# Four loads of GpSimd behind the input's landing, memory attention one step earlier, the closing sum of squares behind the up tile

## What is computed

```python
for i in range(DEPTH):                      # DEPTH = 2
    h = rmsnorm(x, mix_norm[i])
    mem_k, mem_v = split(rmsnorm(mem, mem_norm) @ w_mem_kv[i])
    if i == 0:                              # gated short convolution
        b_gate, c_gate, u, q_mem = split(h @ a_in[0])
        y_main = b_gate * causal_short_conv(c_gate * u, conv_w[0])
    else:                                   # stick-breaking attention over shared k, v
        q_sb, q_mem = split(h @ b_in[0])
        y_main = stick_breaking_attention(q_sb, k_sh, v_sh)
    y_mem = softmax(q_mem @ mem_k.T / 8) @ mem_v          # 4 heads of 64, 256 memory rows
    x = x + concat(y_main, y_mem) @ w_o[i]
    h = rmsnorm(x, ffn_norm[i])
    x = x + (silu(h @ w_gate[i]) * (h @ w_up[i])) @ w_down[i]     # 2816 wide
    if i == 0: k_sh, v_sh = split(rmsnorm(x, kv_norm) @ w_kv_shared)
```

## Time and profile before

| | us |
|---|---|
| median of 3 runs | 1225.7 |
| lowest and highest | 1224.52, 1225.96 |
| the profiled execution | 1227.68 |
| its span | 1226.3 |

### The profile page before, as it was taken

The page is one execution under the profiler, slowest core; times in us unless marked ns, Lnnn a source line. Parts: engine busy times, 40 slices in busy tenths (PEclk is TensorE's granted clock), DMA queues, the critical chain, the costliest instruction groups (busy, mean ns, idle before and its releaser), DMA issues.

```text
span 1226.3 us, 21837 instructions
## 1 busy us (share of the span) xinstructions
PE 1163.0 (95%) x9014; PEld 1114.4 (91%) x9014; DVE 832.8 (68%) x1266; ACT 623.4 (51%) x938; POOL 162.1 (13%) x123
## 2 busy tenths in 40 slices
PE   7999899999898789999999999999999998999996
PEld 6989899999887669999999898989899988999995
DVE  4577677778773656777778657386645767677775
ACT  4645544435563546444445665565436544555553
POOL 1102100000120003000000000000001032433431
PEclk8999999999998979999999999999999997999999
DMA  8545578777643125777887445354325553555540
GB/s 300 166 150 186 182 259 267 241 252 226 244 149 113 61 76 174 256 242 248 275 266 240 169 154 170 121 161 149 121 73 167 183 181 103 172 177 194 180 156 36
DMA packets 60467, 221.90 MB, mean 181 GB/s; under 512 B 6752, under 2 KB 7008, under 8 KB 59984
## 3 DMA queue, kind: packets, MB, share of 16 engines
q1 hardware_dynamic: 59904, 219.06, 54.2%
q10 hardware_dynamic: 288, 1.05, 0.2%
q0 software_dynamic: 176, 0.39, 0.2%
HBM read 219.42 MB, written 1.05 MB: 180 GB/s over the span
## 4 chain that ended last, share of the span: by engine, by line
PE 81%; DVE 10%; ACT 5%; issue 3%; DMA 1%; POOL 0%; SPq 0%; ACTq 0%; DVEq 0%
PE PS L350 23%; PE PS L352 22%; PE PS L351 22%; PE PS L355 13%; DVE w_lo L1310 3%; ACT w_hi L837 2%; DVE PS L1879 1%; DMA ARENA<-memT 1%; ACT ARENA L926 1%; DVE SQ L1577 1%; DVE ARENA L1346 0%; DVE raw L1332 0%; PE PS L453 0%; DVE SQ L1346 0%; DVE ARENA L1493 0%
## 5 line engine op out<-in xcount | busy, mean ns | idle before, releaser
L1310 DVE TENSOR_TENSOR w_lo<-raw,w_hi 128x1024 fp32r<-128x1024 f32 x325 | 398.8, 1227 | 277.1 <-ACT w_hi L837 276.6
L837 ACT ACTIVATE w_hi<-raw 128x1024 fp32r<-128x1024 f32 x356 | 372.8, 1054 | 150.7 <-PE PS L352 122.7
L350 PE MATMUL PS<-Y_hi,w_hi 128*128 128x256 f32 x1240 | 359.4, 290 | 11.8 <-DVE w_lo L1310 4.8
L351 PE MATMUL PS<-Y_lo,w_hi 128*128 128x256 f32 x1240 | 354.8, 286 | 0.0
L352 PE MATMUL PS<-Y_hi,w_lo 128*128 128x256 f32 x1240 | 354.7, 286 | 0.0
L350 PEld LDWEIGHTS PS<-Y_hi,w_hi 128*128 128x128 f32 x1240 | 241.8, 195 | 18.4 <-issue 9.7
L351 PEld LDWEIGHTS PS<-Y_lo,w_hi 128*128 128x128 f32 x1240 | 242.2, 195 | 0.4 <-issue 0.2
L352 PEld LDWEIGHTS PS<-Y_hi,w_lo 128*128 128x128 f32 x1240 | 242.0, 195 | 0.0
L350 PE MATMUL PS<-H_hi,w_hi 128*128 128x256 f32 x808 | 232.2, 287 | 7.2 <-POOL H_lo L1936 2.8
L352 PE MATMUL PS<-H_hi,w_lo 128*128 128x256 f32 x808 | 229.3, 284 | 0.0
L351 PE MATMUL PS<-H_lo,w_hi 128*128 128x256 f32 x808 | 229.3, 284 | 0.0
(11 more groups left out here) (210 smaller groups left out, 1342.7 us busy)
## 6 DMA issues: line engine op xcount, KB each, us to landing
raw<-stream SPq DMA_DIRECT2D x404, 512.0 KB, 4.1
ARENA<-memT SPq DMA_DIRECT2D x2, 512.0 KB, 9.2
X<-xT SPq DMA_DIRECT2D x1, 1024.0 KB, 12.9
ARENA<-c_rows SPq DMA_DIRECT2D x2, 512.0 KB, 7.4
ARENA<-memT SPq DMA_DIRECT2D x1, 1024.0 KB, 9.1
ARENA<-ctxT SPq DMA_DIRECT2D x1, 1024.0 KB, 7.0
outT<-ARENA SPq DMA_DIRECT2D x2, 512.0 KB, 2.6
CROW<-c_rows SPq DMA_DIRECT2D x1, 512.0 KB, 8.3
```

Of the source, the lines that this page charges most:

```text
L350: pe.matmul(o, wh, xh, start=start, stop=False, skip_group_check=True)
L351: pe.matmul(o, wh, xl, start=False, stop=False, skip_group_check=True)
L837: act.activation(w_hi[n % RING][:], raw[at][:], ACT.Copy).then_inc(*mark("hi", n))
L1310: dve.tensor_tensor(w_lo[n % RING][:], raw[raw_of("slot", n)][:], w_hi[n % RING][:], ALU.subtract).then_inc(*mark("lo_dve", n))
```

## The change

The first step of memory attention's wait is taken out on all three engines (TensorE's `nothing(6)` becomes `nothing(5)`, ScalarE and VectorE lose their first empty `yield`); `residual_sum` goes from between the first gate and up tile to behind the up tile, in both layers; GpSimd waits for `x_in` before its four loads. No instruction other than that wait is added, and none is removed.

```diff
@@ memory_attention, TensorE
                 for b in bs:
                     emptied[b] = [("ma_exp", l, 7)]
-                yield from nothing(6)
+                yield from nothing(5)
                 pe.wait_ge(*past("ma_prob", l, 7))
@@ gate_up and ffn, TensorE
-            def gate_up(l, j, ready=None, side=None, between=None):
+            def gate_up(l, j, ready=None, side=None):
                 p = j % 2
                 claim(2 * p, 2 * p + 1)
                 assert n == gate_slot(l, j)
                 tall(PS[:, 2 * p, 0:T], H_of[l], ready)
                 emptied[2 * p] = [("gate", l, j)]
-                if between:
-                    between()
                 if side:
                     side.step()
                 tall(PS[:, 2 * p + 1, 0:T], H_of[l])
@@
             def ffn(l, tail):
-                gate_up(l, 0, [("h_lo", l, k) for k in range(KC)], between=lambda: residual_sum(l))
+                gate_up(l, 0, [("h_lo", l, k) for k in range(KC)])
+                residual_sum(l)
                 gate_up(l, 1)
@@ memory_attention, ScalarE
                 yield
-                yield
                 act.wait_ge(*past("ma_max", l))
@@ pool_program
+            pool.wait_ge(*past("x_in"))
             for i, (dst, src) in enumerate(((mask_sb[:], masks), (scan_m[:], scan_mask), (W2[0:RANK, :], gla_w2[0]),
                                             (W2[32:32 + RANK, :], gla_w2[1]))):
                 pool.dma_start(dst, src).then_inc(*mark("second_in", i, by=16))
```

## The result

| | us |
|---|---|
| before, median of 12 runs | 1225.13 |
| after, median of 12 runs | 1229.67 (1226.52 to 1232.42) |
| after / before | 1.0038, 95% interval 1.0029 to 1.0046 |
| profiled execution of after, its span | 1232.05, 1230.7 |

The change costs 4.5 us by the medians and 4.7 by the ratio (3.6 to 5.6), 4.6 in what follows. Against the profiled execution of before the span of after is 4.4 us longer, at a mean clock of 0.976 against 0.978, so the two profiles can be compared place by place.

What follows compares the result with a forecast made beforehand. TensorE bounds the kernel (81% of the chain that ended last). 5.9 + 5.4 - 1.4 - 0.4 + 0.1 - 1.1 = +8.5 on the median of 1225.7 gives 1234.2 us; range 1228.6 to 1238.4.

Steps and rivals of the forecast that it cites:

- the rival of the kept clock: Feed-forward, both layers: TensorE keeps full clock behind both longer stalls, so 5.4 goes: 1228.8 us; chance 0.13.
- the clock behind the two stalls: Third gate tiles, both layers: matmuls at 1.2 GHz for 5.5 us after each restart, 2.7 each, 5.4 together.
- the gains of the other parts: Start 1.4 off, memory attention layer 0 0.4 off, layer 1 net 0.1 on, stick-breaking groups 1.1 off.
- The stalls of TensorE: Before third gate tiles 2.49 to 5.43 and 1.54 to 4.48; before attention's transposes 1.2 in layer 0, 7.3 in layer 1.
- to read "issue" by the code: Third gate tile, both layers: the wait is for the bank that `G_lo` frees, 0.1 before the tile starts.
- part 1: Closing sum behind the up tile: ScalarE's chain to `G_lo` moves by 2.94 a layer, 5.9 together, plus 5.4 of clock.
- 2.49 kept it and 2.69 did not: TensorE's clock after idle time in before's trace: full speed after 2.49 us, 1.2 GHz after 2.69 (at 1034.21).
- The loads: Start: GpSimd's four loads behind the input's landing let the memory halves and the input land earlier; 1.4 us off.
- Memory attention, layer 1, and the groups: Layer 1: 3.0 lost at the transposes, a 3.0 tile given back, net 0.1 on; groups' tails earlier, 1.1 off.
- The tile came back as said: Stick-breaking groups, layer 1: one tile of 3.0 us fills TensorE's 4.65 us idle gap before the third group's tails.
- the two after them keep their distance: Stick-breaking groups: the tails after the third come at 432.1 instead of 433.25, the next two at unchanged distance; 1.1 off.
- The luck of the clock: Other places, such as 1034.21: the clock may be lost or kept as arrival times shift, up to 2.7 us each way.

Runs made afterwards that it cites:

- the kernel without the sum: Against before: GpSimd's loads wait for the input and memory attention's step is taken out, the closing sum not moved; 0.9964, 4.5 us faster.
- the filled gap: Against before: seven matmuls of constants into a free bank in TensorE's idle time ahead of the third stick-breaking group's tails, nothing moved; 0.9963, 4.5 us faster.
- the filled stall of the feed-forward: Against before: closing sum moved behind the up tile, seven matmuls of constants ahead of the third gate tile, both layers; 1.0045, 5.9 us slower.
- layer 1's filled attention stall: Against before: loads' wait, attention's step out, sum inside first gate tile, fourteen warm-up matmuls, eleven matmuls of constants ahead of layer 1's transposes; 0.9915, 1216.46 us.

## Why the prediction was right, and where its sizes were off

The forecast was +8.5, measured +4.6 (3.6 to 5.6): the sign, the mechanisms and the stalls came as worked out, the time at the lower end of the range. By the time alone the result lies nearest to the rival of the kept clock (1228.8), but the trace refutes it: the windows behind both stalls stand at 0.50, and matmuls there are 0.21 apart. Of the 3.9 us between forecast and result, about 1.4 is the clock behind the two stalls, 5.4 forecast and some 4 measured. About 1.7 are the gains of the other parts, 2.8 forecast and 4.5 measured (loads and attention without the sum). The rest, 0.8, lies within the intervals.

**The stalls of TensorE** were read right to about a tenth where it mattered: 5.43 and 4.48 forecast, 5.37 and 4.42 found; 7.3 against 7.11 in layer 1's attention. In layer 0's attention it was 1.2 against 0.86. The step that carried this was to read "issue" by the code: a claim whose bank comes free 0.1 before the tile starts, twice. After the change the profile itself names `G_lo`.

**The clock behind the two stalls was mis-sized**: 5.4 in the sum of part 1, some 4 measured. The step that failed is the one that took 5.5 us at 1.2 GHz after each restart, from memory attention's stall of 4.24. A stretch at 1.2 GHz costs nothing while TensorE is idle, and here more of it lay in the stall. In layer 0 the clock fell near 136.9 (the mean of 136 to 138 is 0.72, so 0.56 of it, the last 1.1 us, at 0.50) and rose near 143.7 (0.57 in 142 to 144). From the restart at 139.88 that is 3.8 us, which cost 1.67. In layer 1 it rose later, 5.1 us behind the restart, and cost 2.25. The prediction gave a bound of 0 to 5.5 and took a value near the top of it. It also rounded up: at the spacings of the rows, 0.12 and 0.21, its 5.5 us cost 2.4 and not 2.7. One profile is thin ground for such a price: in the kernel with the sum alone, memory attention's stall was 4.13, and the matmuls behind it were slow for 3.0 us instead of 5.5.

**"2.49 kept it and 2.69 did not"** held for the one profile and is no line between the two. The stall of 2.49 at the start of layer 0's feed-forward stands unchanged in eight kernels. Six kept the clock at the restart (one of these lost it 1.5 us later). In the kernel without the sum and in that with the filled gap it lost the clock, in the first of these so:

```profile
136.73 0.55 PE L350 MATMUL PS<-H_hi,w_hi 128*128 128x256 f32 x1 [2.49 <-issue]
```

Two other kernels kept it behind 2.73 and 2.78 us of idle time at the place of 1034.21. So some executions of before may already pay a part of the clock's price.

**The loads**: 1.4 forecast, 1.8 measured, 2.4 in the profile. Between the two profiles the landing moved by 1.3, over all profiles by about 1.0. The further 1.0 of the pair, which came from the clock, is mostly the luck of one execution: the first matmuls are at 2.4 GHz in most kernels that leave the loads alone.

**Memory attention, layer 1, and the groups**: 1.4 forecast for all of the attention, 2.0 (0.9 to 3.8) measured. The tile came back as said, with 1.17 idle before the third tails and these at 1.99. From the first group's tails to the last's it takes 40.3 us in four of five profiles of the old order that have no filler in the gap (38.8 in the fifth). The new order was profiled six times: four times it takes 38.1 to 38.6, so 1.7 to 2.2 less, and in after and in the kernel with the attention alone 36.6 and 35.6. The forecast was 1.1. Its step that "the two after them keep their distance" held in the four (to 0.1 us in three of them) and failed in the two. In the four all three tails behind the third ran slow, in the kernel with layer 1's step alone out so:

```profile
429.34 3.43 PE L355 MATMUL PS<-ARENA,consts 128*128 128x256 f32 x12 [1.38 <-DVE ARENA L1501]
435.56 3.63 PE L355 MATMUL PS<-ARENA,consts 128*128 128x256 f32 x12 [1.94 <-DVE ARENA L1501]
442.00 3.25 PE L355 MATMUL PS<-ARENA,consts 128*128 128x256 f32 x12 [2.80 <-DVE ARENA L1501]
```

In after the second of them was at 2.4 GHz, 1.99 instead of 3.59. So the 3.1 in the bookkeeping holds some luck. TensorE's idle time over attention and groups together is the same in both profiles, 17.97 before and 18.31 after: what was won between them is clock alone, and the matmuls of constants won 4.5 of the same kind without moving anything.

**The luck of the clock** was named with up to 2.7 each way. The profile of after shows one such place, in the second block, which the change doesn't touch. Transposes there, in before, in the kernel with the attention alone, in after, and in the kernel with the sum alone:

```profile
813.30 1.09 PE L594 MATMUL PS<-consts,ARENA 128*128 128x128 f32 x8 [2.55 <-DVE ARENA L1586]
```

```profile
803.10 1.09 PE L594 MATMUL PS<-consts,ARENA 128*128 128x128 f32 x8 [2.57 <-DVE ARENA L1584]
```

```profile
816.27 1.97 PE L593 MATMUL PS<-consts,ARENA 128*128 128x128 f32 x8 [2.56 <-DVE ARENA L1583]
```

```profile
820.50 1.97 PE L595 MATMUL PS<-consts,ARENA 128*128 128x128 f32 x8 [2.57 <-DVE ARENA L1587]
```

Behind 2.55 to 2.57 of idle time the clock was kept in eleven of the thirteen profiles and lost in two; that cost after 1.5 us in its profiled execution. The two are those with the sum moved and its stalls left empty. Whether that is chance or goes with the moved sum, two profiles can't tell.

**What stays open.** The piecewise sum is +5.4 to +6.1 and the whole change +4.6. The intervals are wide enough for this, and no run tells whether something is shared between the parts beyond noise. Each kernel was profiled once, so where a part of a gain is put down to the clock at one place, it rests on single executions.

## What to carry to other kernels

A tiny operation that the bottleneck engine does for others, like this closing sum, is placed by who waits for it: follow the chain behind it to the next claim of the bottleneck engine, and put it as early as its inputs allow; earlier than that, the bottleneck engine waits for it (0.71 us in layer 1 here). A wait that the profile calls "issue" may be a claim of a bank: look in the code for who frees it, and for its end just ahead of the restart. A stall of TensorE costs its length and the slower matmuls behind it; where the stall can't be removed, a few matmuls of constants into a free bank, placed ahead of every wait that they don't need, can keep the clock and take away the second part of the price. They did so in the two feed-forward stalls and in the groups' gap; in layer 1's attention, with 2.37 us left idle, they didn't. Before a price is put on a lost clock, look at several profiles of the place: single ones differed here by up to 3 us in the groups.

## What the runs showed that was not expected

- Seven matmuls whose products nobody reads made the kernel 0.37% faster (0.9963), 4.5 us, with no other instruction moved. The same seven one claim later gained nothing (1.0002).
- Stalls of the same length don't settle whether the clock is lost: idle for 2.55 to 2.57 us at the same place of the program it was kept in before and lost in after, and idle for 2.49 at the start of layer 0's feed-forward it was kept in six kernels and lost in two. A rest of 2.34 in the filled stall of the feed-forward kept it; one of 2.37 in layer 1's filled attention stall didn't. The Trainium skill, "TensorE: Matmul & The Clock Gate", Part 1, has the monitor behind the clock run free of the program; these rows agree with it.
- When the clock falls within a stall of TensorE, an earlier fall was the cheaper one in after's two stalls: the stretch at 1.2 GHz behind the restart was 3.8 us where the clock had fallen 3 us before the restart, and 5.1 us where it had fallen about 1.6 us before it.
